# Sample attention: value pages issued from SyncE, behind the keys of the next sample

## The reference

```python
def fox_sample(q, k, v, logf, cache_k, cache_v, cache_logf, page_table):
    kp = cache_k[page_table].reshape(DB, past, H, Dh)
    vp = cache_v[page_table].reshape(DB, past, H, Dh)
    ...
    s_past = jnp.einsum('bqhd,bkhd->bhqk', q, kp).astype(jnp.float32) * scale
    s_past = s_past + suffix[:, :, None, :] + cn[:, :, :, None]
    ...
    p = jax.nn.softmax(jnp.concatenate([s_past, s_new], axis=-1), axis=-1)
    o = (jnp.einsum('bhqk,bkhd->bqhd', p[..., :past].astype(v.dtype), vp)
         + jnp.einsum('bhqk,bkhd->bqhd', p[..., past:].astype(v.dtype), v))
```

## Time and profile before

| | |
|---|---|
| three executions | 1959.45, 1962.62, 1966.36 us; median 1962.62 |
| profiled execution, span | 1963.6 us |
| PE busy | 1861.1 us, 95% of the span |
| DVE, ACT, POOL busy | 599.5, 296.4, 191.5 us |
| mean granted clock of PE | 0.973 of 2.4 GHz |
| DMA | 407.03 MB, mean 207 GB/s |
| key pages and value pages | 128 each of 256.0 KB, median 6.7 and 7.3 us from issue to landing |

### The profile page before, as it was taken

One profiled execution on the slowest core, in us unless ns is written; L12 is line 12 of the kernel. 1 busy time (PEld: TensorE's weight loads), 2 busy tenths in 40 slices (PEclk: granted clock), 3 DMA queues, 4 the chain that ended last, 5 costly groups with the idle time before them and its releaser, 6 DMA issues. The chain is left out here.

```text
span 1963.6 us, 22843 instructions
## 1 busy us (share of the span) xinstructions
PE 1861.1 (95%) x8445; PEld 967.2 (49%) x8445; DVE 599.5 (31%) x1414; ACT 296.4 (15%) x514; POOL 191.5 (10%) x276
## 2 busy tenths in 40 slices
PE   8999999799999989998999997999999999996996
PEld 4454454456666555665555444544444444442442
DVE  4201124333433344553232224411111111110687
ACT  2000001122222222332110112300000000000000
POOL 2000004100000003333000000100000000000231
PEclk9999999899999998999999997999999999998898
DMA  7111110622122028999421244699999999997232
GB/s 273 16 33 57 46 49 1 245 96 70 45 91 64 30 87 290 370 382 342 177 69 66 75 177 167 241 350 425 422 420 417 429 418 418 421 424 276 90 130 96
DMA packets 108384, 407.03 MB, mean 207 GB/s; under 512 B 17433, under 2 KB 35418, under 8 KB 95986
## 3 DMA queue, kind: packets, MB, share of 16 engines
q1 hardware_dynamic: 83474, 327.59, 43.1%
q0 software_dynamic: 16496, 56.15, 7.8%
q10 hardware_dynamic: 8304, 21.84, 2.8%
HBM read 354.74 MB, written 50.79 MB: 207 GB/s over the span
## 5 line engine op out<-in xcount | busy, mean ns | idle before, releaser
L2102 PE MATMUL psum<-arena 128*64 128x512 f32 (+1 forms) x1024 | 341.1, 595 | 1.4 <-DVE arena L2196 1.4
L848 PE MATMUL psum<-arena 128*128 128x363 f32 (+1 forms) x768 | 255.7, 478 | 4.3 <-ACT arena L879 4.3
L2102 PEld LDWEIGHTS psum<-arena 128*64 128x64 f32 (+1 forms) x1024 | 129.0, 163 | 179.1 <-issue 177.3
L848 PEld LDWEIGHTS psum<-arena 128*128 128x128 f32 x768 | 140.6, 192 | 78.6 <-ACT arena L879 6.8
L2141 PE MATMUL psum<-arena 128*64 128x512 f32 (+1 forms) x512 | 170.0, 595 | 1.0 <-DVE arena L2210 1.0
L2141 PEld LDWEIGHTS psum<-arena 128*64 128x64 f32 (+1 forms) x512 | 66.1, 163 | 101.9 <-issue 101.9
L2448 PE MATMUL psum<-arena 128*128 128x512 f32 x256 | 113.8, 602 | 1.4 <-DVE arena L2485 1.4
L1563 PE MATMUL psum<-arena 128*128 128x512 f32 x256 | 113.0, 596 | 1.6 <-PEq L1398 1.6
L300 PE MATMUL psum<-arena 128*128 128x512 f32 x256 | 112.0, 594 | 0.0
L2196 DVE TENSOR_TENSOR arena<-psum,g_moe_rows 128x1024 f32<-128x1024 f32 x24 | 29.4, 1225 | 250.7 <-PE psum L2096 250.7
L1099 PE MATMUL psum<-ident,arena 128*128 128x128 f32 x512 | 82.2, 296 | 14.9 <-PEq L740 4.1
(11 more groups left out here) (289 smaller groups left out, 1946.6 us busy)
## 6 DMA issues: line engine op xcount, KB each, us to landing
arena<-in_w_exp_gate SPq DMA_DIRECT2D x32, 2048.0 KB, 13.5
arena<-in_w_exp_up SPq DMA_DIRECT2D x32, 2048.0 KB, 13.9
arena<-in_w_exp_down SPq DMA_DIRECT2D x32, 2048.0 KB, 10.5
arena<-in_cache_k SPq DMA_DIRECT2D x128, 256.0 KB, 6.7
arena<-in_cache_v POOLq DMA_DIRECT2D x128, 256.0 KB, 7.3
moe_out<-arena ACTq DMA_DIRECT2D x24, 512.0 KB, 11.9
arena<-in_w_in SPq DMA_DIRECT2D x5, 2048.0 KB, 19.9
moe_out<-arena SPq DMA_DIRECT2D x1, 10240.0 KB, 35.0
```

The lines of the kernel that those rows point to most:

```text
L848: done = mm(c.bank[7][:, 0:b - a], WG[blk % 2][:, k, q * P:(q + 1) * P], HT[:, k, a:b], start=(k == 0), stop=(k == KD - 1))
L2102: last = mm(out[rows_, :], XT[:, u % 2, k, rows_], c.ring_tile(LOAD[kind, u, r])[:, k, :], start=(k == 0), stop=(k == KD - 1))
```

## The change

POOL keeps its three clears and issues no value pages. SP gets a function `load_values(b)`, which for each chunk reads four page numbers, waits for `v_used` and issues the four transfers. It is called for sample 0 behind the first bias transfers, for sample b-1 behind the keys of sample b from b = 2 on, and for the last sample after the loop, ahead of the merge weights.

```diff
         def _(sp):
+            def load_values(b):
+
+                for ch in range(NCH):
+                    numbers = c.page_numbers(sp, b, ch)
+                    if b >= 1:
+                        sp.wait_ge(v_used, NCH * (b - 1) + ch + 1)
+                    for g in range(CH):
+                        sp.dma_start(VC[:, ch, g, :], c.cache_v[bass.ds(numbers[g] * P, P), :]
+                                     ).then_inc(v_in[ch], 16)
+
...
                 if b == 0:
+                    load_values(0)
                     continue
                 for ch in range(NCH):
                     sp.wait_ge(k_tr, U * (b - 1) + NPAIR * (ch + 1))
                     c.load_keys(sp, b, ch)
+                if b >= 2:
+                    load_values(b - 1)
+            load_values(DB - 1)
             for n, w in enumerate((c.w_up_a, c.w_up_b)):
                 sp.dma_start(view(c, UP_AT + n * WBLK, KF, D), w).then_inc(c.up_in, 16)
...
-            pool.wait_ge(c.pages_in, 16)
-            for b in range(DB):
-                numbers = [c.page_numbers(pool, b, ch) for ch in range(NCH)]
-                for ch in range(NCH):
-                    if b >= 1:
-                        pool.wait_ge(v_used, NCH * (b - 1) + ch + 1)
-                    for g in range(CH):
-                        pool.dma_start(VC[:, ch, g, :], c.cache_v[bass.ds(numbers[ch][g] * P, P), :]
-                                       ).then_inc(v_in[ch], 16)
```

## The result

The changed kernel takes 2059.07 us (2056.96 to 2063.32, four runs), the kernel before beside it 1963.59 us (1959.45 to 1966.36): a ratio of 1.0488 (95% interval 1.0468 to 1.0509), 95.5 us slower. Predicted were 2064 us and 102 us more.

The account below looks back on a forecast made before the run. PE bounds sample attention before the change; SP's issuing, at 1.15 us a page, bounds it after. Line and landing 94.9, merge weights 6 and tail 1 make +102 us on the 1962.6 median: 2064 us, range 2047 to 2081.

Parts of the forecast that it names:

- The bound: Sample attention: SP's issuing line sets the time without waiting, 38.2 us a sample against 22.3 for PE.
- The page price: SP's time to issue one key or value page in sample attention, taken as 1.15 us for 240 pages.
- the lower bound of 1.085: Lowest SP price in us a page, from a burst of 16 key pages issued in 15.00 us without hiccups.
- The landing: End of sample attention: the last value page lands 4.0 us after its start at 1020.5, at 1024.5 us.
- The merge weights: Start of the merge stage: weights issued behind the last values on SP expose a wait, taken as +6 us.
- the three prices: Exposed wait for the merge weights, by three assumed transfer times: 3.5, 8.2 or 18 us.
- The clock: PE pauses in sample attention may lower its granted clock; nothing charged in the beat, about 1 us in the tail.
- The 1 us for the tail: PE work after the last value, partly at the lower clock: about 1 us added.
- The sum: Whole kernel: 94.9 + 6 + 1 = +102 us, giving 2064 us on the median.
- The gain at the start: Start of sample attention: PE's 3.16 us wait for sample 1's keys eases, but is lost as keys issue 18 us later.
- Rival B: Sample attention: values behind keys remove PE waits and the half clock, so the kernel gets faster, 1954 us; chance 0.01.
- Rival A: Sample attention: SP has room, value issue hides behind PE's beat, no change at 1963 us; chance 0.02.

Follow-up runs that it names:

- run 1: The changed kernel, but values of samples 1 to 7 reuse the page numbers read for their keys, transfers and order unchanged: 2007.79 us, ratio 1.0234.
- run 2: The kernel before, but SP reads four more page numbers behind each chunk of keys and does not use them: 2005.44 us, ratio 1.0220.
- run 6: The kernel before with merge weights issued at the stage's start and one of four value chunks on SP, the rest on GpSimd: 1988.97 us, ratio 1.0127.
- run 7: The kernel before with merge weights issued at the stage's start and two of four value chunks on SP, the rest on GpSimd: 2010.66 us, ratio 1.0232.
- run 12: The kernel before with two of four value chunks on SP and the merge weights behind the last keys: 2001.74 us, ratio 1.0195.
- run 4: The changed kernel with the two merge weights issued at the start of the stage, ahead of the bias: 2054.31 us, ratio 1.0469.
- run 10: The kernel before, with GpSimd's values of sample 0 held back until SP has issued the same chunk of sample 1's keys: 1960.10 us, ratio 0.9988.
- run 11: The kernel before, but for sample 0 GpSimd reads four page numbers and issues four values in turn: 1961.52 us, ratio 0.9992.

## Why the prediction was right

- **The bound.** SP's line without waits, as written: 0.8 us of waiting, a beat of 37.4 us (predicted 38.2). Runs 1 and 2, which change instructions and no transfer, moved the time by -51 and +43 us; that is what shows it. The DMA share was forecast near 0.6 and was 0.72, the rate near 220 GB/s and was 227.
- **The page price**, the largest term. I took 1.15 us; SP's line from the end of the first bias row (734.73) to the last value issue (1014.96) is 280.2 us, less 9.9 of bias and 0.8 of waits, over 240 pages: 1.12. The 1.16 came from a stretch in which the DMA engines stood at a share of 0.96, and the 1.18 from two chunks alone, too few for an average; at a share of 0.72 the price lay midway between 1.16 and the lower bound of 1.085. 240 x 0.03 = 6 us: the line ended at 1015.0 and not 1020.8. The prediction's "so the hiccups don't come from a full DMA" rested on those two chunks, and runs 6, 7 and 12, with 1.15 to 1.18 at shares of 0.85 to 0.91, speak against it.
- **The landing** of the last values took 5.4 us from its start (1014.6 to 1020.0) and not 4.0. With no weights behind them, in run 4, it took 4.1 (1016.0 to 1020.1), so the weights right behind are the likely cause. Together: +90.3 and not +94.9.
- **The merge weights**: +5.7 us against +6 predicted; run 4 got 4.8 back by moving them. The nearness is partly luck: the three prices spanned 3.5 to 18 us, and the choice between the first two was a guess. By their own times (1033 and 1038, less 1029.7) the first two are 3.3 and 8.3, and the best slice of the page is 429 GB/s, not 424; neither changes the sum.
- **The clock**: it fell in pauses and cost nothing in the beat, as predicted. PE's idle time was 10 us a sample and not 16, since its own work grew to 27.3 us (21.3 before). The 1 us for the tail can't be told apart from the rest.
- **The sum**: 102 predicted, +96.0 at the start of the merge, 95.5 between the medians. Most of the difference is the page price and the landing, 94.9 for 90.3.
- **The gain at the start** was lost, as predicted: PE waited 11.26 us for the keys of sample 1, up to 762.26, where it had waited 3.16. The prediction laid that wait to the burst of values. In run 10, with the values held back, waits for these keys stayed, so the burst is not all of it. Rival B's price for the start (5.7 us) is neither shown nor refuted, since runs 10 and 11 moved the pause and didn't remove it.
- **Rival A** (room on SP) needed 0.65 us a page. Even with four pages a sample moved the time rose by 12.6 us over its base.

## What to carry to other kernels

Before moving transfers to another issuer, count that engine's instructions for each, reads of page numbers included, and compare the sum with the beat of the stage; an engine that shows no busy time can be 90% full. When PE "waits for DMA" while the DMA share falls and landings get quicker, as here, look first whether the issuer is late. And behind a moved group look at what stood behind it: the place of a large load in a queue decides what waits for it.

## What I had not expected of the hardware

- Two 2 MB loads ahead of a 16 KB transfer in the same queue held it up so that PE waited 16.75 us; moving them out of the busy end of the stage cost 13 us instead of gaining some.
- An issue with only a register move of 29 ns ahead of it isn't as cheap as the issue's own duration: 0.56 us a page in run 1 for an instruction with a median of 0.38.
- The price of a page on SP was higher where the DMA engines were fuller: 1.12 us at a share of 0.72, 1.15 and 1.17 at 0.85 (runs 7 and 12), 1.18 at 0.91 (run 6), though 1.16 at 0.96 in the kernel before. Why was not tried.
